# Four gate projections of the next branch set around the mean, the variance and the norm of the last retention head

## What is computed

```python
z = u @ w_in                                   # zq, zkv, zpe, rq, rk, rv, rg, cq, ck, cv, zg
o_b, state = retention(q_b, k_b, v_b, state)   # 4 heads, per-token causal, in chunks
def head_group_norm(o, g):                     # per head, over its 128 values
    mu = mean(o); var = mean((o - mu)**2)
    return (o - mu) * rsqrt(var + EPS) * g
y_b  = head_group_norm(o_b, g_ret_gn) * silu(rg)
br_b = y_b @ w_br_b                            # 512 -> 1024
gates = sigmoid(zg + b_gate)                   # 3 branches x 1024 channels
merged = gates[0] * br_a + gates[1] * br_b + gates[2] * br_c
x = x + rms_norm(merged @ w_out, g_post_mix)
```

## Time and profile before

| | us |
|---|---|
| median of three runs | 2771.71 |
| lowest and highest run | 2769.47, 2781.54 |
| the profiled execution | 2778.73 |
| span of its trace | 2776.9 |

### The profile page before, as it was taken

How to read it: one execution, slowest core, us unless ns; L and a number is a source line. 1 busy time by engine, 2 the same in 40 slices (tenths; PEclk the granted TensorE clock), 3 DMA queues, 4 the chain that set the end, 5 groups by cost and what they waited for, 6 DMA issues and landing times.

```text
span 2776.9 us, 46587 instructions
## 1 busy us (share of the span) xinstructions
PE 2558.4 (92%) x17836; PEld 2417.4 (87%) x17836; DVE 1467.9 (53%) x2244; ACT 796.3 (29%) x1428; POOL 827.0 (30%) x335
## 2 busy tenths in 40 slices
PE   8889999999989899999788999899999898999996
PEld 7679888988978799999677898798899787999995
DVE  4771564364564845336757516634635647354266
ACT  4342122244334311111224421223433333111112
POOL 3113223222323234333221232132223232333342
PEclk9899999999999999999889999899999999999997
DMA  4112112222222122222121121132222221222222
GB/s 143 39 42 84 54 48 86 66 86 85 80 66 92 49 84 84 84 82 80 60 85 31 57 84 46 40 94 75 82 84 77 65 88 54 79 82 83 83 84 80
DMA packets 65687, 204.73 MB, mean 74 GB/s; under 512 B 7936, under 2 KB 16000, under 8 KB 65360
## 3 DMA queue, kind: packets, MB, share of 16 engines
q10 hardware_dynamic: 47808, 174.08, 20.2%
q1 hardware_dynamic: 17680, 27.90, 3.0%
HBM read 190.93 MB, written 11.03 MB: 73 GB/s over the span
## 4 chain that ended last, share of the span: by engine, by line
PE 79%; DVE 11%; DVEq 6%; issue 2%; ACT 1%; DMA 0%; SPq 0%; ACTq 0%
PE job L354 66%; PE outp L402 4%; PE scores L382 3%; DVE rstd L1025 3%; DVEq L1052 2%; PE scores L277 1%; PE turn L392 1%; DVEq L1088 1%; PE job L363 1%; DVE arena L1016 1%; DVE rstd L1033 1%; DVEq L1189 1%; DVE x L1053 1%; DVEq L1031 1%; PE job L547 0%
## 5 line engine op out<-in xcount | busy, mean ns | idle before, releaser
L354 PE MATMUL job<-arena,w_hi 128*128 128x288 f32 (+1 forms) x9984 | 1817.4, 304 | 46.0 <-DVE q L1190 16.7
L354 PEld LDWEIGHTS job<-arena,w_hi 128*128 128x128 f32 x9984 | 1501.4, 192 | 89.0 <-issue 36.3
L647 POOL TENSOR_TENSOR w_lo<-raw,w_hi 128x1024 fp32r<-128x1024 f32 x331 | 826.8, 2498 | 1918.0 <-ACT w_hi L666 1918.0
L354 PE MATMUL job<-arena,w_lo 128*128 128x288 f32 (+1 forms) x4992 | 1090.6, 298 | 0.0
L354 PEld LDWEIGHTS job<-arena,w_lo 128*128 128x128 f32 x4992 | 820.4, 191 | 0.0
L666 ACT ACTIVATE w_hi<-raw 128x1024 fp32r<-128x1024 f32 x331 | 349.6, 1056 | 1079.1 <-PE job L354 910.2
L999 DVE TENSOR_TENSOR tmp<-job,rstd 128x576 f32<-128x576 f32 x70 | 52.9, 756 | 295.6 <-PE job L354 295.3
L402 PEld LDWEIGHTS outp<-probT,v 128*128 128x128 f32 x992 | 129.9, 192 | 65.5 <-ACT probT L759 53.8
L402 PE MATMUL outp<-probT,v 128*128 128x128 f32 x992 | 152.1, 284 | 30.0 <-DVE arena L1096 21.0
L277 PE MATMUL scores<-q,const 128*128 128x288 f32 (+1 forms) x296 | 100.8, 480 | 69.3 <-ACT q L727 60.2
L988 DVE CAST arena<-tmp 128x576 fp32r<-128x576 f32 x64 | 151.7, 2370 | 4.7
(11 more groups left out here) (152 smaller groups left out, 1763.0 us busy)
## 6 DMA issues: line engine op xcount, KB each, us to landing
raw<-in_w ACTq DMA_DIRECT2D x332, 512.0 KB, 3.5
bias<-in_bias SPq DMA_DIRECT2D x16, 256.0 KB, 2.7
x<-in_x SPq DMA_DIRECT2D x4, 576.0 KB, 8.7
cs<-in_rope SPq DMA_DIRECT2D x4, 576.0 KB, 4.5
out_o_bandk<-k SPq DMA_DIRECT2D x8, 288.0 KB, 3.0
out_o_bandv<-tmp SPq DMA_DIRECT2D x8, 288.0 KB, 3.3
out_y<-x SPq DMA_DIRECT2D x1, 2304.0 KB, 6.9
bias<-in_mem SPq DMA_DIRECT2D x8, 256.0 KB, 3.6
```

Of the source, the lines that this page charges most:

```text
L354: mm = pe.matmul(ps[0:m, po:po + nn], w[:, s, c:c + m], x[:, k, so:so + nn], start=(k == 0 and w is WHI and x is hl[0]), stop=(k == kt - 1 ...
L647: nc.gpsimd.tensor_tensor(WLO[:, u % RING, :], RAWS[:, u % RAW, :], WHI[:, u % RING, :].bitcast(F32), ALU.subtract).then_inc(lo_done, 1)
```

## The change

In the last head of a layer, too, a projection now stands between mean and variance: gate 1. Two more projections, gates 2 and 3, stand between the variance and the wait for the normed head, which is now ahead of the branch's outputs 0 to 3 without a gate between them. From output 4 on the branch goes as before. Four gates are then alive at once, so gates 1 to 3 have tiles of their own, `COS`, `SIN` (both in the tile `cs`) and `Q[:, 0]`, whose contents are no longer read at this point. The four memsets, which clear parts of the same tiles, move behind output 3. The signal that the head is normed moves ahead of the two store requests, and the wait for the stores moves between the evictions of gates 2 and 3. ScalarE's program and the order of the units follow.

```diff
+        GATES_EARLY = TMP[:, 0], COS, SIN, Q[:, 0]
...
                     for e2 in range(KT // 2):
-                        for e in range(ahead if e2 == 0 else 0, 2):
-                            project(unit(), KT, U_HL)
+                        for e in (2 * e2, 2 * e2 + 1):
+                            if e >= ahead:
+                                project(unit(), KT, U_HL)
...
                         plain(ONES, RO)
-                        if filler:
-                            project(unit(), KT, U_HL)
+                        project(unit(), KT, U_HL)
                         wait_ready()
                         plain(ONES, rstd2[:, :])
-                branch(wait_ready, ahead=1)
+                for _ in range(2):
+                    project(unit(), KT, U_HL)
+                branch(wait_ready, ahead=4)
...
                 def branch(b, after=None, ahead=0):
+                    first = n["job"] - ahead
                     for e in range(KT):
+                        gate = GATES_EARLY[e] if b == 1 and e < ahead else TMP[:, e % 2]
                         if e >= ahead:
                             place()
                             n["job"] += 1
-
-                        evicted()
-                        act.activation(TMP[:, e % 2], TMP[:, e % 2], ACT.Sigmoid,
+                            evicted()
+                        else:
+                            act.wait_ge(job_free, l * JOBS + first + e + 1 + 2)
+                        act.activation(gate, gate, ACT.Sigmoid,
                                        bias=g_col("b_gate", b * KT + e)).then_inc(gate_done, 1)
...
-                        if filler:
-                            placed()
+                        placed()
                         n["job"] += 1
                         n["gate"] += 1
                         root(rstd2[:, :])
-                branch(1, ahead=1)
+                placed()
+                placed()
+                branch(1, ahead=4)
...
-                            scale_job(TMP[:, 0])
+                            scale_job(GATES_EARLY[0])
...
                             scale_job(K[:, 0, 0:NT])
+                        else:
+                            scale_job(GATES_EARLY[1])
...
                 norm_head(RET_HEADS - 1)
                 finish(RET_HEADS - 1)
+                is_ready(v.tensor_copy(small[:, 12:13], small[:, 13:14]))
                 store()
                 store()
-                is_ready(v.tensor_copy(small[:, 12:13], small[:, 13:14]))
-                dve.drain()
+                scale_job(GATES_EARLY[2])
                 wait_stores()
                 dve.sem_inc(phase_done, 1)
-                for b in range(2):
-                    v.memset(Q_EVEN[BAND_HD:P, b], 0.0)
-                    v.memset(Q_ODD[0:BAND_HD, b], 0.0)
-                branch(False, ahead=1)
+                scale_job(GATES_EARLY[3])
+
+                def clear_queries(e2):
+
+                    if e2 == 1:
+                        for b in range(2):
+                            v.memset(Q_EVEN[BAND_HD:P, b], 0.0)
+                            v.memset(Q_ODD[0:BAND_HD, b], 0.0)
+
+                branch(False, clear_queries, ahead=4, early=GATES_EARLY)
...
-        branch(1, a["w_br_b"][l])
+        branch(1, a["w_br_b"][l], ahead=4)
```

More of the change, by code:

```diff
@@ L534, in _ @@
                         r0, r1 = j * RET_DK, (j + 1) * RET_DK
-                        filler = j == 0 or p + 1 < RET_HEADS // 2
                         turn_values(chunks, but=4)
@@ L1118, in merged, with branch @@
                     is_ready(lows(lambda i: M[:, i], None, U_HL, k, k + 2))
-                def branch(first, after=None, ahead=0, last=False):
+                def branch(first, after=None, ahead=0, last=False, early=()):
                     for e in range(KT):
+                        gate = early[e] if e < len(early) else TMP[:, e % 2]
                         if e % 2 == 0:
-                            for j in range(0 if e else ahead, 2):
-                                scale_job(TMP[:, j])
+                            for j in range(2):
+                                if e + j >= ahead:
+                                    scale_job(TMP[:, j])
                             if last and e == KT - 2:
@@ L1133, in branch @@
                         if first:
-                            free(v.tensor_tensor(halves(M[:, e]), job_halves(s), halves(TMP[:, e % 2]), ALU.mult))
+                            free(v.tensor_tensor(halves(M[:, e]), job_halves(s), halves(gate), ALU.mult))
                         else:
-                            v.tensor_tensor(halves(TMP[:, e % 2]), job_halves(s), halves(TMP[:, e % 2]), ALU.mult)
+                            v.tensor_tensor(halves(gate), job_halves(s), halves(gate), ALU.mult)
                             dve.drain()
-                            free(v.tensor_tensor(M[:, e], M[:, e], TMP[:, e % 2], ALU.add))
+                            free(v.tensor_tensor(M[:, e], M[:, e], gate, ALU.add))
                         if e % 2:
@@ L1657, with branch @@
         cols = lambda c: w_tile(w[:, c:c + P])
-        def branch(b, wb):
+        def branch(b, wb, ahead=0):
+            for e in range(ahead):
+                add(cols(zg + b * D + e * P))
             for e in range(0, KT, 2):
-                add(cols(zg + b * D + e * P))
-                add(cols(zg + b * D + (e + 1) * P))
+                if e >= ahead:
+                    add(cols(zg + b * D + e * P))
+                    add(cols(zg + b * D + (e + 1) * P))
                 add(w_tile(wb[:, e * P:(e + 1) * P]), w_tile(wb[:, (e + 1) * P:(e + 2) * P]))
```

## The result

| | before | after |
|---|---|---|
| median of nine runs, us | 2778.31 | 2757.67 |
| lowest and highest | 2769.47, 2787.24 | 2750.52, 2762.07 |
| the profiled execution | 2778.73 | 2750.68 |

The ratio is 0.9927, with a 95% interval of 0.9909 to 0.9946, so the change gains 20 us (15 to 25). Forecast were 18.2 us and 2753.5 us. The median of before had been 2771.71 us over the first three runs and is 2778.31 over nine.

A forecast was written before the change was run, and what follows sets the result against it. TensorE, busy 92% of the span, was taken as the bound, losing waits and clock at the retention stage's end. Per layer 10.08 + 25.60 = 35.68 us against 44.79 saves 9.1, 18.2 in both: 2771.71 becomes 2753.5 us, range 2745 to 2764.

The forecast's parts named there:

- What bounds the place: End of retention stage: TensorE loses time to waits (4.4 us layer 1, some 4.8 layer 2) and low clock (6.2 us).
- the sum: From mean's start to fourth output: 44.79 us becomes 35.68, gaining 9.1 us a layer, 18.2 in both.
- Mean, projection, variance: Last head, mean's start to variance's end with gate 1 between: 10.08 us, ends 8.57 and 11.7.
- The upper end of 11.7: Upper end for mean, projection and variance: 10.08 us with a second loss of 1.5 us on top.
- The packed part: Behind the variance, gates 2 and 3 and four outputs take 25.60 us if TensorE never waits.
- The chain: Last head's norm, variance to signal: 10.2 us (8.8 to 12.4) against 12.8 us of cover.
- Rival D: Norm chain outgrows its cover, 13.4 us against 12.8: up to 0.9 us wait a layer, 2755.3 us; chance 0.05.
- The moved steps: Store wait, memsets (2.6 us), sigmoids and weights move and stay hidden; gate 1's eviction wait of 0.29 us goes.
- B: Clock stays up in the last head's mean: stretch 34.17 us, 21.2 us gained, 2750.5 us; chance 0.12.
- C: Waits go but the clock's loss stays at 6.2 us: 9.2 us gained, 2762.5 us; chance 0.12.
- F: Clock stays low through the packed work: 2819 us; decides if low for over 21 us; chance 0.04.
- E: Gain given back behind the stretch at an unmoving load or store wait: 2771.7 us; chance 0.05.

The follow-up runs named there:

- the repeat: The changed kernel measured and profiled again, unaltered: median 2759.37 us, ratio 0.9940 to the kernel before.
- gate 1 alone: Changed kernel with gate 1 between mean and variance but nothing behind the variance; gates 2 and 3 after outputs 0 and 1: 2782.74 us, 1.0020 to before.
- the longer chains: Two kernels: changed kernel with the last head's norm chain 4.6 or 9.6 us longer by repeated inversion: 2762.26 us (0.9947) and 2775.54 us (0.9992 to before).
- VectorE's order alone: Kernel before with only VectorE reordered: signal ahead of stores, gate 1 evicted before the store wait, memsets behind output 3; 2773.20 us, 0.9969 to before.
- cover for the long link alone: Changed kernel with gates 1, 2 and 3 all behind the variance, nothing between mean and variance: 2764.19 us, 0.9945 to before.
- five gates: Changed kernel with one more gate: gate 1 ahead of the mean, gate 2 between the sums, 3 and 4 behind the variance; 2745.93 us, 0.9883 to before.
- one gate behind the variance: Changed kernel with only gate 2 behind the variance, gate 3 coming after outputs 0 and 1: 2760.89 us, 0.9927 to before.

## Why the prediction was right

**What bounds the place.** The two losses were those named. The waits of the variance, the first output and gate 1's eviction are gone, the mean's is left. (The last of the three stood ahead of the second output, not of the first one's second half, as the prediction calls it; the sum is the same.) Of the 16.6 us, 9.2 are waits (TensorE's idle time in the two windows of the earlier trace rows) and the other 7.3 clock, where the sum had 18.2 less 9.2, so 9.0. The 1.7 us that lack are in the next two terms.

**Mean, projection, variance.** This term was mis-sized a little: 10.08 us was taken from the other heads, and it is 11.33 and 10.07, and 10.07 and 11.29 in the repeat. In one layer of each profile the clock stays low for about twice as long as in the heads of the earlier trace rows. The low level is half of the full one, so 0.74 over 11.33 us is 5.9 us at the low level, and 0.85 over 10.07 is 3.0. The upper end of 11.7 had that case. It costs 1.2 us per execution.

**The packed part.** 25.81 and 25.82 us against 25.60. By VectorE's rows above the two gates take 12.92 us and the first output 3.29, the other three 3.20 each as in the earlier trace rows; the 0.2 us a layer lie where one kind of job follows another.

**The chain.** It took 8.6 us, just under the lower end of 8.8 to 12.4. The weight subtraction fell beside the inversion, which did not suffer (3.75 us), and the multiplication took 0.82 in both layers of both profiles of the change. The prediction did not say where the subtraction would fall, and it missed the multiplication by 0.4 us only. Rival D did not come; the kernels with gate 1 alone and with the longer chains show the meeting with GpSimd that would have fed it (2.87 and 2.90 us for the multiplication).

**The moved steps.** Gate 3's eviction, the store wait, the memsets, the sigmoids and the weights cost nothing: no wait names them. VectorE's order alone did not shorten the stretch beyond what differs between executions, so the signal's earlier place is no hidden part of the gain.

**The rivals.** B did not happen in either profile of the change: what changed from layer to layer was how long the low stretch lasted, not whether it came. C and F are out by the clock of 1.00 behind the variance, E by TensorE's later matmuls, which keep the 6.35 us. What the clock still takes, with the 0.2 us of the packed part in it, is 37.14 - 34.17 = 3.0 us and 1.7, not C's 6.2, and the 5.9 us at the low level are far from the 21 of F's condition.

**The time.** 2757.67 us against 2753.5, inside the range. The 4 us between them come from the base: the median of before moved up by 6.6 us between three runs and nine, and the gain by medians is 20.6 us, 2.4 more than forecast. The gain, 20 us with an interval of 15 to 25, and 17 us in the repeat, holds the forecast. That it lies above the 16.6 us of the stretch in the first profiles is not the mechanism's doing but lies within the scatter between executions.

## What to carry to other kernels

A chain of small dependent steps at the end of a stage is hidden as a whole only when independent matrix work stands behind each of its hand-overs. Cover for the short link alone just moved the wait to the long one, and here lost 10 us; cover for the long link alone won 10 of the 16.6. Count the chain and its cover in microseconds (8.6 against 12.8) and look what the queue behind it must still do, the evictions above all, before deciding how many tiles to pull forward. Where the times scatter by more than the effect, measure the same stretch of equal work in several profiles of each kernel.

## What the hardware showed that was not expected

The same 48 matmuls at a granted clock of 1.00 take 6.24 or 6.40 us, one or the other through a whole feed-forward part, and which one changes from execution to execution in both kernels. What decides it was not found.

The clock can drop without a wait: with five gates TensorE was busy throughout and yet ran at 0.51 from 1779.0 to 1782.5 us, behind the short matmuls of the head's output. In layer 1 the same matmuls stand there, and the clock is 1.00 throughout.

The same wait costs clock in one place and none in another: with one gate behind the variance TensorE idles for 2.36 us in layer 1 and 2.37 in layer 2, and behind that it runs at 1.00 and at 0.73 over 6.40 us. So the price of a wait in clock, which was more than half of the loss here, can be forecast only as a range.
